# Hybrid conv and RWKV-7 layer on one core: key sums and low-rank products in fp32r pieces, and a later place for some weight remainders on VectorE

## The chip, the cores and the metric

The kernel runs on one core of a Trainium2 chip. The metric is the device time of one execution in microseconds. The profile is one execution of the program, with the engines TensorE (PE, its weight loads as PEld), VectorE (DVE), ScalarE (ACT), GpSimd (POOL) and SyncE (SP).

## The reference

One layer with 512 tokens, 16 learned meta tokens ahead of them (T = 528), model width 2048. All arithmetic is float32.

```python
h = rms_norm(concat([meta, x]), norm_mix_g)
p = h @ w_in                                   # 2048 -> 3072 conv columns + 3360 RWKV columns
y_conv = b_gate * conv3(c_gate * xc)           # 1024 channels
r, k, v, wd, ad, gd = split(token_shift(p[..., 3072:], mu))
w = -softplus(-(w0 + tanh(wd) @ w2)) - 0.5     # second low-rank stage: 64 -> 1024
decay = exp(-exp(w))
a = sigmoid(a0 + ad @ a2)                      # second low-rank stage: 64 -> 1024
g = sigmoid(gd) @ g2                           # 160 -> 1024
kk = k * k_k
kk = kk / max(norm(kk over each head of 64), 1e-12)
k = k * (1 + (a - 1) * k_a)
y = wkv7_scan(r, decay, k, v, -kk, kk * a)     # state S of 64 x 64 per head
y = (group_norm(y) * lnx_w + lnx_b + sum(r * k * r_k) * v) * g
h_res = h_res + concat([y_conv, y]) @ w_out
h_res = h_res + relu(rms_norm(h_res) @ w_up)**2 @ w_down
out = rms_norm(h_res)[meta tokens dropped]
```

## The kernel before

Features lie on the 128 partitions, tokens along the free dimension. Every dense product is made of three fp32r products: weights and activations are each cut into a rounded part (`w_hi`, `act_hi`) and a remainder (`w_lo`, `act_lo`), and TensorE adds hi·hi, hi·lo and lo·hi (`dense`, L1494). Small products (`ss`, `low`, `vtr`, gram and the rest) are plain fp32, which shows as two records each.

The 16 RWKV heads are worked off in 8 pairs (`pair(j)`, j = 0 to 7). While TensorE runs the dense projections of the next pair (six tiles of 16 k-steps, 96 k-steps in all, one k-step being three products of 528 columns), it runs the small steps of the present pair in between. `PACE` (L74) gives the order of the steps and how many k-steps stand ahead of each; the running totals that matter here are ss 2, low 7, vtr 12, ahead0 18, gram0 25, tr 28, gram1 31, and at the end var 93, ahead6 96.

Every engine walks the same list of steps in program order. At a step it does its own operations of that step and then the weight work that the total calls for: one quarter (4 k-steps of weights, 128 x 512) for each 4 k-steps. A quarter goes through three hands. SyncE loads it to `w_raw`, which holds 4 quarters (`load`, L447: the load of quarter q waits until the remainder of quarter q-4 is made). ScalarE rounds it to `w_hi` (`split`, L753). VectorE makes the remainder `w_lo` (`split`, L1063). In the text q5, q6, ... are the quarters of a pair, counted so that the dense work of the pair begins with q0; the engines run 6 quarters ahead, so that step "low" has the split of q6, "vtr" those of q7 and q8, "ahead0" q9, "gram0" q10 and q11, and "ahead6" the q5 of the next pair. For the steps in `SPLIT_FIRST` (low, base1, base2, y, var) an engine does the splits ahead of its operations, for the others behind; ScalarE has gram0 among the former too:

```python
            for name, k in zip(PACE, schedule()):
                if name not in ACT_SPLIT_FIRST:
                    steps_of(name)
                while splits < (96 if last and name == "var" else k) // KQ:
                    split(Q_PAIR + LEAD + splits, 24, j)
                    splits += 1
                if name in ACT_SPLIT_FIRST:
                    steps_of(name)
```

The steps around the change, in the names of the code:

- `ss`: squares of the keys (`fsq`, made by ScalarE in `square_keys`, L797) are summed over each head by a product with `same_head` (L1567, two halves of 264 columns). VectorE takes the sums (`ssm`, L1157), ScalarE the root, VectorE the reciprocal (L1160).
- `low`: the decay and learning-rate projections, four products with 64 rows each (L1573), one on the upper and one on the lower half of the array. ScalarE takes sigmoids (L861, L862), VectorE goes on with the scan (L1164) and what follows it.
- `vtr`: v is turned (L1578). VectorE does `kkn`, `tfac`, `kp` (L1176 to L1179).
- `ahead0`: VectorE scales the operands `at`, `b`, `bt`, `rt`, `kt` (L1182 to L1189).
- `gram0`: TensorE waits for `rt` (L1590). VectorE makes `rb` (L1191) and masks the result (`NA`, L1195). ScalarE rounds `rb` to `rb_hi` (`rbh`, L879), behind its splits of q10 and q11. GpSimd subtracts (`rbl`, L648) and masks `NA` (L653).
- `tr`: TensorE waits for the masked `NA`, turns bt and kt (L1595), then waits for `rbl` and sums `rb_hi` and `rb_lo` (L1598, L1599).
- `var`: variance and gate products (L1701, L1704), ScalarE's root (L913), VectorE's last four operations of the pair.

GpSimd loads the small weights of the next pair by its own DMA queue: `wa_w` once the products of `low` are done (L624, L625), `g_w` at the end of a pair. After the pairs come the output projection, the MLP and the final norm, which take about two thirds of the time and which the change leaves alone.

Of the kernel before, what the change touches and what calls it, by code (L numbers as in the profile page):

```python
# [31 lines left out]
P = 128  # L32
# [164 lines left out]
N_CONST = 4 + 6 + 4 + 5 + 3 + 4 + 2  # L197


def hybrid_layer(nc, x, meta, norm_mix_g, w_in, shift_mu, conv_w, decay_w0, decay_w2, iclr_a0, iclr_a2,  # L200
# [32 lines left out]
    same_head = sb("same_head", [P, P])  # L233
# [28 lines left out]
    KA = m_sb("KA", [P, 2, SLOTS, 2, C])  # L262
    AMV = m_sb("AMV", [P, 2, SLOTS, P])
    v_tok = m_sb("v_tok", [P, SLOTS, P])
    b_tok = m_sb("b_tok", [P, SLOTS, P])
    k_tok = m_sb("k_tok", [P, SLOTS, P])
# [9 lines left out]
    low_wa = m_sb("low_wa", [P, T])  # L276
    low_r = lambda name, n: sb(name, [P, n], F32R, on=mix)
    low_hi, low_lo, low_tail = low_r("low_hi", SEQ), low_r("low_lo", SEQ), low_r("low_tail", SEQ)
    wa_w = m_sb("wa_w", [P, P])
# [3 lines left out]
    rb_lo = low_r("rb_lo", SEQ)  # L283
# [8 lines left out]
    over_states.close()  # L292
    ZB = m_sb("ZB", [P, 7, P])
# [236 lines left out]
    def _(pool):  # L530
# [41 lines left out]
        const(nc.gpsimd.tensor_copy(same_head[:], blocks[:, 2, :]))  # L572
# [53 lines left out]

        def load_g(j):
# [4 lines left out]
        def pair(j, last=False):  # L632
# [7 lines left out]
            if not last:  # L640
                pool.wait_ge(pe_done, step(PE_STEPS, "low", j))
                load_wa(j + 1)

            if last:
                pool.wait_ge(z_done, at(6, 3, j))
                load_y(0, 1)
            pool.wait_ge(act_done, step(ACT_STEPS, "rbh", j))
# [12 lines left out]
            else:  # L660
                pool.wait_ge(dve_done, step(DVE_STEPS, "y4", j))
# [55 lines left out]
    def _(act):  # L717
# [86 lines left out]
        for n in range(6):  # L804
# [16 lines left out]
            if n == 1:  # L821
                act.wait_ge(z_done, 2)
                nc.scalar.activation(low_wa[0:HS, :], low_wa[0:HS, :], ACT.Tanh).then_inc(low_done, 1)
            if n == 2:
                act.wait_ge(z_done, 3)
                nc.scalar.activation(low_g[:, META:T], low_g[:, META:T], ACT.Sigmoid).then_inc(low_sig, 1)
                act.wait_ge(low_sig, 2)
# [12 lines left out]
        def pair(j, last=False):  # L840
# [13 lines left out]
            def steps_of(name):  # L854
# [56 lines left out]
                if name == "var":  # L911
                    pe("var")
# [921 lines left out]
```

## Time and profile before

| | |
|---|---|
| time, median of 3 runs | 2428.42 us (2427.71 to 2428.54) |
| the profiled execution's own time | 2427.97 us |
| its span | 2426.1 us |
| PE busy | 2401.2 us (99%) |
| PEld, DVE, ACT, POOL busy | 2034.1, 1130.0, 787.9, 206.5 us |
| TensorE's granted clock over the span | 0.997 |
| first `ss` of pairs 0 and 7 | 93.43 and 735.65 us |

The span runs from the first to the last instruction. The sum of the prediction is made against the profiled execution's own time. Starts of TensorE's instructions tell more than their durations here, since matmuls overlap and their ends are modelled.

### The profile page before, as it was taken

To read this page: it belongs to the slowest core of one execution; us is meant where nothing else is said; L and a number is where in the kernel's file an instruction comes from. 1 tells how busy PE (TensorE), PEld (TensorE's weight loads), DVE (VectorE), ACT (ScalarE), POOL (GpSimd) and SP (SyncE) were. 2 spreads that over 40 slices of the span, in tenths; PEclk is the share of its full clock that TensorE was granted. 3 is DMA by queue.
4 is the path that set the end of the run, shared out by engine and by line. 5 is a ranking of instruction groups with operands and counts; after the bars stand their busy time and mean duration, and the time that the engine had idled before them with its cause. 6 is when DMAs were issued, how large, how long until landed. Compare 5 with 4: busy or idle time off the path is not lost.

```text
span 2426.1 us, 42112 instructions
## 1 busy us (share of the span) xinstructions
PE 2401.2 (99%) x16524; PEld 2034.1 (84%) x16524; DVE 1130.0 (47%) x1733; ACT 787.9 (32%) x1329; POOL 206.5 (9%) x249
## 2 busy tenths in 40 slices
PE   8999999999999999999999999999999999999997
PEld 8999999999998788888888888888888888888886
DVE  7557657657657644433333333333332333333343
ACT  6534434434434322322222222221322322222333
POOL 6101101001002322000000000000000000000032
PEclk9999999999999999999999999999999999999998
DMA  8344244244244632333233333333332332332232
GB/s 248 81 98 103 68 101 103 69 105 101 70 102 116 190 107 79 96 105 96 82 110 92 90 97 96 88 105 87 87 108 84 99 101 84 100 104 87 87 100 92
DMA packets 487454, 243.68 MB, mean 100 GB/s; under 512 B 83294, under 2 KB 481120, under 8 KB 486880
## 3 DMA queue, kind: packets, MB, share of 16 engines
q1 hardware_dynamic: 470064, 219.99, 32.8%
q0 software_dynamic: 6720, 18.45, 2.4%
q10 hardware_dynamic: 10496, 2.62, 0.6%
q8 instruction: 145, 2.38, 0.4%
q14 instruction: 29, 0.24, 0.0%
HBM read 224.08 MB, written 16.92 MB: 99 GB/s over the span
## 4 chain that ended last, share of the span: by engine, by line
PE 89%; DVE 7%; ACT 1%; issue 1%; DMA 1%; SPq 0%; ACTq 0%; DVEq 0%
PE PD L1512 68%; PE PD L1517 13%; PE PD L1728 1%; DVE uni L1160 1%; DVE uni L1286 1%; DVE w_lo L1065 1%; PE PD L1541 1%; PE PW L1541 1%; PE PW L1690 1%; PE PW L1590 0%; PE PD L1446 0%; PE PW L1595 0%; DVE uni L1164 0%; PE PW L1654 0%; PE PW L1696 0%
## 5 line engine op out<-in xcount | busy, mean ns | idle before, releaser
L757 ACT CAST w_hi<-w_raw 128x512 fp32r<-128x512 f32 x780 | 457.6, 620 | 700.8 <-PE PD L1512 525.7
L1065 DVE TENSOR_TENSOR w_lo<-w_raw,w_hi 128x512 fp32r<-128x512 f32 x780 | 548.5, 736 | 293.0 <-ACT w_hi L757 289.8
L1512 PE MATMUL PD<-act_lo,w_hi 128*128 128x512 f32 x1344 | 531.3, 395 | 0.0
L1512 PE MATMUL PD<-act_hi,w_hi 128*128 128x512 f32 x1344 | 529.1, 394 | 0.0
L1512 PE MATMUL PD<-act_hi,w_lo 128*128 128x512 f32 x1344 | 528.6, 393 | 0.0
L1512 PE MATMUL PD<-u_hi,w_hi 128*128 128x512 f32 x1024 | 409.7, 400 | 0.0
L1512 PE MATMUL PD<-u_hi,w_lo 128*128 128x512 f32 x1024 | 403.3, 394 | 0.0
L1512 PE MATMUL PD<-u_lo,w_hi 128*128 128x512 f32 x1024 | 401.5, 392 | 0.0
L1512 PEld LDWEIGHTS PD<-act_hi,w_hi 128*128 128x128 f32 x1344 | 252.5, 188 | 61.7 <-issue 1.4
L1512 PEld LDWEIGHTS PD<-act_lo,w_hi 128*128 128x128 f32 x1344 | 252.1, 188 | 58.3 <-issue 0.2
L1512 PEld LDWEIGHTS PD<-act_hi,w_lo 128*128 128x128 f32 x1344 | 252.8, 188 | 57.3
L1418 DVE TENSOR_TENSOR res<-PD,res 128x512 f32<-128x512 f32 x128 | 88.5, 692 | 413.3 <-PE PD L1512 413.3
L1517 PE MATMUL PD<-act_hi,w_hi 128*128 128x264 f32 (+1 forms) x1248 | 266.2, 294 | 0.0
L1517 PE MATMUL PD<-act_hi,w_lo 128*128 128x264 f32 (+1 forms) x1248 | 251.3, 283 | 0.0
L1517 PE MATMUL PD<-act_lo,w_hi 128*128 128x264 f32 (+1 forms) x1248 | 251.1, 282 | 0.0
L1512 PEld LDWEIGHTS PD<-u_hi,w_lo 128*128 128x128 f32 x1024 | 192.2, 188 | 50.1
L1512 PEld LDWEIGHTS PD<-u_lo,w_hi 128*128 128x128 f32 x1024 | 192.3, 188 | 45.0
L1512 PEld LDWEIGHTS PD<-u_hi,w_hi 128*128 128x128 f32 x1024 | 192.3, 188 | 43.7
L1402 DVE SCALAR_TENSOR_TENSOR nt<-PD,rs 128x512 f32<-128x512 f32 x64 | 44.3, 692 | 366.5 <-PE PD L1512 366.2
L985 ACT ACTIVATE nt<-nt 128x512 f32<-128x512 f32 x64 | 40.6, 634 | 513.0 <-DVE nt L1402 513.0
L1517 PEld LDWEIGHTS PD<-act_hi,w_hi 128*128 128x128 f32 x1248 | 193.2, 189 | 12.6 <-issue 6.7
L1517 PEld LDWEIGHTS PD<-act_hi,w_lo 128*128 128x128 f32 x1248 | 192.2, 188 | 0.0
(319 smaller groups left out, 1880.5 us busy)
## 6 DMA issues: line engine op xcount, KB each, us to landing
w_raw<-in_w_up SPq DMA_DIRECT2D x256, 256.0 KB, 3.2
w_raw<-in_w_down SPq DMA_DIRECT2D x256, 256.0 KB, 2.9
w_raw<-in_w_in SPq DMA_DIRECT2D x200, 256.0 KB, 3.1
w_raw<-in_w_out SPq DMA_DIRECT2D x64, 256.0 KB, 2.7
residual<-res POOLq DMA_DIRECT2D x2, 2048.0 KB, 10.1
out<-rows SPq DMA_DIRECT2D x8, 512.0 KB, 5.3
yin<-mixed POOLq DMA_DIRECT2D x15, 256.0 KB, 3.6
x_rows<-in_x SPq DMA_DIRECT2D x3, 1024.0 KB, 7.4
```

The lines of the kernel that those rows point to most:

```text
L757: nc.scalar.copy(w_hi[:, q % RING], w_raw[:, q % RAW]).then_inc(hi_split, 1)
L985: nc.scalar.activation(nt, nt, ACT.Square).then_inc(u_sq, 1)
L1065: V.tensor_tensor(w_lo[:, q % RING], w_raw[:, q % RAW], w_hi[:, q % RING].bitcast(F32), ALU.subtract).then_inc(lo_split, 1)
L1160: done("inv", V.reciprocal(fsq, fsq))
L1286: done("inv2", V.reciprocal(ysq, ysq))
L1402: V.scalar_tensor_tensor(nt1[:, m % 3, :], pd_seq(n), 0.0, rs1[:], ALU.max, ALU.mult).then_inc(evacuated[n % 2], 1)
L1418: V.tensor_tensor(res[:, m, :], pd_seq(n), res[:, m, :], ALU.add).then_inc(evacuated[n % 2], 1)
L1512: ins = M(pd_seq(n), w, v[:, k, first:first + SEQ], start=begin, stop=end)
L1517: ins = M(PD[:, 2 * (n % 2) + a, cols], w, v[:, k, start:start + cols.stop - cols.start], start=begin, stop=end)
L1541: ins = M(bank[:, h, cols], w, v[:, k, start:start + cols.stop - cols.start], start=begin, stop=end)
L1690: ins = M(PW[:, (c - 1) % 2, 0:P], GT[:, c - 1, :], HB[:, 0, :] if c == 1 else ZB[:, c - 2, :], start=True, stop=True)
L1728: ins = M(PD[:, OUT_BANK[t], :], w, v[:, k, 0:SEQ], start=(k == 0 and i == 0), stop=(k == KT - 1 and i == 2))
```

## The change

The squared keys are cut into a rounded part `k_sq_hi` (ScalarE, right behind the square) and a remainder `k_sq_lo` (GpSimd, `split_squares`), and `ss` becomes four fp32r products with `same_head_r` in the place of two fp32 ones. ScalarE's `square_keys` for the next pair moves from step ahead6 to step var, ahead of the root. The plain `same_head` constant goes.

The low-rank weights `wa_w` are cut by GpSimd (`split_wa`, a cast and a subtraction of 128 x 128 for each pair, between the load of the next weights and `rbl`), the low-rank activations once at the start (`low_wa_hi` by ScalarE, `low_wa_lo` by VectorE), and `low` becomes twelve fp32r products in the place of four fp32 ones. `wa_w`, `rb_lo`, `k_sq_hi`, `k_sq_lo` and `low_wa` lie over other tiles of the mix, and ScalarE's `ktok` gets a wait on `wa_split` for that.

VectorE's splits move: q5 of the next pair from ahead6 to behind the operations of the next pair's `ss`, and q7 and q8 from behind `vtr` to behind the operations of `ahead0`, where q9 already was.

```diff
         def square_keys(j):
             act.wait_ge(z_done, at(5, 3, j))
             nc.scalar.activation(fsq, zk[:], ACT.Square, scale=p_("k_k", j)).then_inc(k_squared, 1)
+            act.wait_ge(k_squared, j + 1)
+            nc.scalar.copy(k_sq_hi[:], fsq).then_inc(k_sq_rounded, 1)
...
+        def split_squares(j):
+            pool.wait_ge(k_sq_rounded, j + 1)
+            nc.gpsimd.tensor_tensor(k_sq_lo[:], fsq, k_sq_hi[:].bitcast(F32), ALU.subtract).then_inc(k_sq_split, 1)
+
+        def split_wa(j):
+            pool.wait_ge(wa_loaded, 32 * (j + 1))
+            nc.gpsimd.tensor_copy(wa_hi[:], wa_w[:]).then_inc(wa_rounded, 1)
+            pool.wait_ge(wa_rounded, j + 1)
+            nc.gpsimd.tensor_tensor(wa_lo[:], wa_w[:], wa_hi[:].bitcast(F32), ALU.subtract).then_inc(wa_split, 1)
...
             if not last:
                 pool.wait_ge(pe_done, step(PE_STEPS, "low", j))
+                pool.wait_ge(wa_split, j + 1)
                 load_wa(j + 1)
...
+            if not last:
+                split_wa(j + 1)
             pool.wait_ge(act_done, step(ACT_STEPS, "rbh", j))
             done("rbl", nc.gpsimd.tensor_tensor(rb_lo, ld[:, 0:SEQ], rb_hi.bitcast(F32), ALU.subtract))
...
             if last:
                 load_y(*range(6, KT - 1))
             else:
+                split_squares(j + 1)
                 pool.wait_ge(dve_done, step(DVE_STEPS, "y4", j))
...
                     done("btok", nc.scalar.copy(b_tok[:].rearrange("p c n -> p (c n)"), in_row(0)))
+                    if not last:
+                        act.wait_ge(wa_split, j + 2)
                     done("ktok", nc.scalar.copy(k_tok[:].rearrange("p c n -> p (c n)"), in_row(1)))
...
                 if name == "var":
+                    if not last:
+                        square_keys(j + 1)
                     pe("var")
                     done("std", nc.scalar.activation(ysq, PW[:, 0, :], ACT.Sqrt, bias=eps_t[:, 1:2]))
-                if name == "ahead6" and not last:
-                    square_keys(j + 1)
...
-            splits, tiles, y_split = 0, 0, 0
+            splits, tiles, y_split = -1 if j else 0, 0, 0
             for name, k in zip(PACE, schedule()):
                 if name not in SPLIT_FIRST:
                     steps_of(name)
-                while splits < (96 if last and name == "var" else k - 4 if last and name in ("amv", "ahead5") else k) // KQ:
+                held = 2 if name == "vtr" else 1 if name == "ahead6" and not last or last and name in ("amv", "ahead5") else 0
+                while splits < (96 if last and name == "var" else k) // KQ - held:
                     split(Q_PAIR + LEAD + splits, 24, j)
                     splits += 1
...
                 if name == "ss":
-                    pe.wait_ge(k_squared, j + 1)
-                    for a in range(2):
-                        ins = M(PW[:, 2 + a, 0:HALF], same_head[:], half(fsq, a), start=True, stop=True)
+                    for i, (made, squares) in enumerate(((k_sq_rounded, k_sq_hi), (k_sq_split, k_sq_lo))):
+                        pe.wait_ge(made, j + 1)
+                        for a in range(2):
+                            ins = M(PW[:, 2 + a, 0:HALF], same_head_r[:], half(squares[:], a), start=(i == 0), stop=(i == 1))
                 if name == "low":
-                    pe.wait_ge(wa_loaded, at(32, 32, j))
+                    pe.wait_ge(wa_split, j + 1)
                     dve("ssm")
                     for a in range(2):
-                        for h in range(2):
-                            ins = M(PW[:, 2 * h + a, 0:HALF], wa_w[hs[h], :], half(low_wa[hs[h], :], a), start=True, stop=True)
+                        for i, (w, v) in enumerate(((wa_hi, low_wa_hi), (wa_lo, low_wa_hi), (wa_hi, low_wa_lo))):
+                            for h in range(2):
+                                ins = M(PW[:, 2 * h + a, 0:HALF], w[hs[h], :], half(v[hs[h], :], a), start=(i == 0), stop=(i == 2))
```

## Rows read from the trace of the kernel before

**Rows 1.** The page's first part: busy time, share of the span, instructions.

```profile
PE 2401.2 (99%) x16524; PEld 2034.1 (84%) x16524; DVE 1130.0 (47%) x1733; ACT 787.9 (32%) x1329; POOL 206.5 (9%) x249
```

**Rows 2.** Timeline of PE in pair 0: start, duration, instruction, output and inputs.

```profile
93.19 0.40 PE L1517 MATMUL PD<-act_hi,w_lo 128*128 128x260 f32 x2
93.43 1.05 PE L1567 MATMUL PW<-uni,same_head 128*128 128x264 f32 x4
...
94.56 0.40 PE L1517 MATMUL PD<-act_lo,w_hi 128*128 128x260 f32 x2
...
97.65 0.39 PE L1517 MATMUL PD<-act_hi,w_lo 128*128 128x260 f32 x2
...
99.41 0.40 PE L1517 MATMUL PD<-act_lo,w_hi 128*128 128x260 f32 x2
```

**Rows 3.** Timeline of PE, the first `ss` of pairs 1 and 2.

```profile
184.81 0.83 PE L1567 MATMUL PW<-uni,same_head 128*128 128x264 f32 x3
...
276.61 0.83 PE L1567 MATMUL PW<-uni,same_head 128*128 128x264 f32 x3
```

**Rows 4.** Waits in pair 1 (184.8 to 214 us): total us, times, longest.

```profile
PEld PW L1590 <- DVE ar L1188: 0.3, 1, 0.3
PEld PW L1595 <- DVE NA L1195: 0.3, 1, 0.3
```

**Rows 5.** Timeline of PE in pair 1, around step `tr`.

```profile
208.45 0.77 PE L1595 MATMUL PW<-ident,bt 128*128 128x128 f32 x5
...
209.84 0.40 PE L1599 MATMUL PW<-rb_lo,same_head_r 128*128 128x512 f32 x1
```

**Rows 6.** Timeline of DVE, one row of pair 0, then pair 1; idle before in brackets.

```profile
107.82 1.29 DVE L1065 TENSOR_TENSOR w_lo<-w_raw,w_hi 128x512 fp32r<-128x512 f32 x2 [1.84 <-ACT w_hi L757]
...
187.74 0.69 DVE L1065 TENSOR_TENSOR w_lo<-w_raw,w_hi 128x512 fp32r<-128x512 f32 x1
...
199.03 0.71 DVE L1179 TENSOR_TENSOR uni<-zk,uni 128x528 f32<-128x528 f32 x1
200.55 1.29 DVE L1065 TENSOR_TENSOR w_lo<-w_raw,w_hi 128x512 fp32r<-128x512 f32 x2 [0.81 <-ACT w_hi L757]
201.76 0.70 DVE L1182 SCALAR_TENSOR_TENSOR ar<-uni 128x528 f32<-128x528 f32 x1
...
205.45 0.69 DVE L1065 TENSOR_TENSOR w_lo<-w_raw,w_hi 128x512 fp32r<-128x512 f32 x1
...
206.84 1.56 DVE L1195 TENSOR_TENSOR NA<-PW,gram_mask 128x640 f32<-128x640 f32 x2
208.43 2.22 DVE L1065 TENSOR_TENSOR w_lo<-w_raw,w_hi 128x512 fp32r<-128x512 f32 x2
```

**Rows 7.** Timeline of ACT in pair 1, and at `var` of the same pair.

```profile
199.83 1.15 ACT L757 CAST w_hi<-w_raw 128x512 fp32r<-128x512 f32 x2
...
204.28 0.62 ACT L757 CAST w_hi<-w_raw 128x512 fp32r<-128x512 f32 x1 [1.24 <-DMA w_raw<-in_w_in]
206.84 0.62 ACT L879 CAST rb_hi<-uni 128x512 fp32r<-128x512 f32 x1 [1.94 <-DVE uni L1191]
...
273.19 0.69 ACT L913 ACTIVATE uni<-PW,eps_t 128x512 f32<-128x512 f32 x1 [2.30 <-PE PW L1704]
```

**Rows 8.** Timeline of POOL in pair 1.

```profile
191.34 0.53 POOL L625 DMA_DIRECT2D wa_w<-in_iclr_a  x1
207.55 1.28 POOL L648 TENSOR_TENSOR rb_lo<-uni,rb_hi 128x512 fp32r<-128x512 f32 x1 [15.69 <-ACT rb_hi L879]
208.79 4.40 POOL L653 TENSOR_TENSOR uni<-NA,level_mask 128x320 f32<-128x320 f32 x4
```

**Rows 9.** DMA issues of the whole program: KB each, median us to landing.

```profile
wa_w<-in_iclr_a POOLq DMA_DIRECT2D x8, 32.0 KB, 2.9
```

**Rows 10.** Two POOL lines: duration in ns, minimum, median, maximum, and forms.

```profile
L573 POOL CAST same_head_r<-blocks x1: 290/290/290, 15.3 to 15.3; 128x128 fp32r<-128x128 f32 x1
...
L653 POOL TENSOR_TENSOR uni<-NA,level_mask x32: 881/1141/1373, 116.3 to 763.1; 128x320 f32<-128x320 f32 x32
```

More of the change, by code:

```diff
@@ L196 @@
 T_END = T_MLP + FFG * 24
-N_CONST = 4 + 6 + 4 + 5 + 3 + 4 + 2
+N_CONST = 4 + 6 + 4 + 4 + 3 + 4 + 2
 def hybrid_layer(nc, x, meta, norm_mix_g, w_in, shift_mu, conv_w, decay_w0, decay_w2, iclr_a0, iclr_a2,
@@ L232, in hybrid_layer @@
     ones = sb("ones", [P, P])
-    same_head = sb("same_head", [P, P])
     same_head_r = sb("same_head_r", [P, P], F32R)
@@ L262, in hybrid_layer @@
     KA = m_sb("KA", [P, 2, SLOTS, 2, C])
+    over_pairs = ExitStack()
+    k_sq_lo = sb("k_sq_lo", [P, T], F32R, on=over_pairs)
+    over_pairs.close()
+    over_pairs = ExitStack()
+    low_wa = sb("low_wa", [P, T], on=over_pairs)
+    over_pairs.close()
     AMV = m_sb("AMV", [P, 2, SLOTS, P])
     v_tok = m_sb("v_tok", [P, SLOTS, P])
+    over_b = ExitStack()
+    rb_lo = sb("rb_lo", [P, SEQ], F32R, on=over_b)
+    over_b.close()
     b_tok = m_sb("b_tok", [P, SLOTS, P])
+    over_k = ExitStack()
+    wa_w = sb("wa_w", [P, P], on=over_k)
+    over_k.close()
     k_tok = m_sb("k_tok", [P, SLOTS, P])
@@ L275, in hybrid_layer @@
     cu = m_sb("cu", [P, T + 2])
-    low_wa = m_sb("low_wa", [P, T])
     low_r = lambda name, n: sb(name, [P, n], F32R, on=mix)
     low_hi, low_lo, low_tail = low_r("low_hi", SEQ), low_r("low_lo", SEQ), low_r("low_tail", SEQ)
-    wa_w = m_sb("wa_w", [P, P])
+    low_wa_hi, low_wa_lo = low_r("low_wa_hi", T), low_r("low_wa_lo", T)
+    wa_hi, wa_lo = low_r("wa_hi", P), low_r("wa_lo", P)
     g_w = m_sb("g_w", [P, P])
@@ L282, in hybrid_layer @@
     g_hi, g_lo, g_tail = low_r("g_hi", P), low_r("g_lo", P), low_r("g_tail", P)
-    rb_lo = low_r("rb_lo", SEQ)
     ar = m_sb("ar", [P, 2, TP])
@@ L292, in hybrid_layer @@
     over_states.close()
+    over_last_states = ExitStack()
+    k_sq_hi = sb("k_sq_hi", [P, T], F32R, on=over_last_states)
+    over_last_states.close()
     ZB = m_sb("ZB", [P, 7, P])
@@ L354, in hybrid_layer @@
     wa_loaded, g_loaded = sem("wa_loaded"), sem("g_loaded")
+    wa_rounded, wa_split = sem("wa_rounded"), sem("wa_split")
     low_done, low_sig, low_top = sem("low_done"), sem("low_sig"), sem("low_top")
@@ L358, in hybrid_layer @@
     z_done, k_squared, key_made = sem("z_done"), sem("k_squared"), sem("key_made")
+    k_sq_rounded, k_sq_split = sem("k_sq_rounded"), sem("k_sq_split")
     conv_step = sem("conv_step")
@@ L680, in _ @@
         load_g(0)
+        split_wa(0)
+        split_squares(0)
         for j in range(PAIRS - 1):
@@ L822, in _ @@
                 act.wait_ge(z_done, 2)
-                nc.scalar.activation(low_wa[0:HS, :], low_wa[0:HS, :], ACT.Tanh).then_inc(low_done, 1)
+                nc.scalar.activation(low_wa[0:HS, :], low_wa[0:HS, :], ACT.Tanh).then_inc(low_sig, 1)
+                act.wait_ge(low_sig, 2)
+                nc.scalar.copy(low_wa_hi[:], low_wa[:]).then_inc(low_top, 1)
             if n == 2:
@@ L826, in _ @@
                 nc.scalar.activation(low_g[:, META:T], low_g[:, META:T], ACT.Sigmoid).then_inc(low_sig, 1)
-                act.wait_ge(low_sig, 2)
+                act.wait_ge(low_sig, 3)
                 nc.scalar.copy(low_hi[:], low_g[:, META:T]).then_inc(low_top, 1)
@@ L1124, in _ @@
                 V.tensor_tensor(low_tail[r, :], low_g2[r, META:T], low_tail[r, :].bitcast(F32), ALU.subtract).then_inc(low_done, 1)
+                dve.wait_ge(low_top, 2)
+                V.tensor_tensor(low_wa_lo[:], low_wa[:], low_wa_hi[:].bitcast(F32), ALU.subtract).then_inc(low_done, 1)
             if n == 4:
-                dve.wait_ge(low_top, 2)
+                dve.wait_ge(low_top, 3)
                 V.tensor_tensor(low_lo[:], low_g[:, META:T], low_hi[:].bitcast(F32), ALU.subtract).then_inc(low_done, 1)
```

1 line of the change is left out of this document (removed).

## The prediction

> **What bounds the kernel.** I read the busy shares first: PE is busy for 2401.2 of 2426.1 us [rows 1], so only what TensorE issues, or a new wait of TensorE, can move the time. Its starts come next, because the ends of matmuls are modelled. In the dense work two products of 260 and 256 columns start 0.24 us apart from the next two (93.19 to 93.43) [rows 2], or 0.119 us for each; this holds through nearly all of a pair. Then I looked for the places where TensorE just meets another engine. Pair 0 takes 184.81 - 93.43 = 91.38 us, pair 1 takes 276.61 - 184.81 = 91.80 us [rows 2, 3]. Both have the same instructions, so pair 1 holds 0.42 us of waiting that pair 0 lacks. The waits name the places: gram0's weight load waits for VectorE's `rt`, and tr's for the masked `NA` [rows 4]. So VectorE between the scan and `NA` is on the edge of being the bound in every pair but the first, and any change of 0.1 us on TensorE or VectorE counts there. The last look is at the timelines of VectorE, ScalarE and GpSimd in pair 1 [rows 6 to 8].
>
> **ss on TensorE.** The fp32 form starts at 93.43 and the second dense group behind it at 94.56 [rows 2]; less the 0.24 us of the first dense group, it costs 0.89 us. Four fp32r products of 264 columns continue the dense pattern at 0.119 us x 264/258 = 0.122 us each, 0.49 us. Gain 0.40 us in each pair. Its inputs: the cast of `k_sq_hi` (some 0.62 us, as ScalarE's cast of a quarter) and the square (0.7) now run where ScalarE waits 2.30 us for the products of var [rows 7], so they are hidden; without that cover they would delay the root by 1.3 us. GpSimd's subtraction takes about 1.3 us (`rbl` [rows 8]). From 270.89, where that wait began, the three end near 273.6, and `ss` starts at 276.61 [rows 3]: a margin of 3 us hides them.
>
> **low on TensorE.** From 97.65 to 99.41, less two dense groups of 0.24 us, the fp32 form costs 1.28 us [rows 2]. Its eight records run two by two, the upper and the lower half of the array together, four times 0.22 us as in ss, so 0.40 us is entry and exit. Twelve fp32r products run as six couples: 6 x 0.122 + 0.40 = 1.13 us, a gain of 0.16. No row shows fp32r products of 64 rows. If they don't overlap they cost 12 x 0.122 + 0.40 = 1.86, a loss of 0.58. I take the couples, since the nearest rows are fp32 products of the same shape that do overlap. Together TensorE is 0.56 us shorter in each pair, 0.02 us longer at the other bound.
>
> **The moved remainders: what comes earlier.** q5 now goes behind ss: `ssm` starts at 187.74 rather than 0.6 us later, which keeps low, now reached 0.40 us earlier, free of a wait. The reciprocal also ends 0.6 us earlier, but q5 and q6 then stand ahead of `ld`, one split more than q6 alone, and a second split costs 1.29 - 0.69 = 0.60 us [rows 6]. So from the scan on nothing is earlier or later. At vtr, `kp` ends at 199.74 and VectorE waits 0.81 us for ScalarE's cast of q7 before it makes q7 and q8 and gets to `at` at 201.76 [rows 6]. Without these two, `at` starts at 199.77. From `at` to the split behind `kt` the five operations take 205.45 - 201.76 = 3.69 us, so that split, now of q7, starts at 203.46; `rt` is ready 2 us earlier and gram0's wait is gone. Two splits at 0.61 us, then the stretch of one split and `rb` ahead of the masks (206.84 - 205.45 = 1.39) and the masks' 1.56 follow: `NA` starts at 206.07 and ends at 207.63 instead of 208.40, and tr can start 0.77 us earlier.
>
> **The moved remainders: what comes later.** `w_raw` holds four quarters, so the load of q11 waits for the remainder of q7. Before, q7's split starts at 200.55 and the cast of q11 at 204.28, where ScalarE had waited 1.24 us for that very DMA [rows 6, 7]: 3.73 us from the one to the other. Now q7's split starts at 203.46, so the cast of q11 starts at 207.19. At gram0 ScalarE does its splits first, so `rbh` is queued behind this cast: it starts 0.53 us later (two casts take 1.15, one 0.62 [rows 7]), 207.72, and ends 208.34, where it was 207.46. `rbl` follows with its old lag of 0.09 and its 1.28 us [rows 8]: 209.71. TensorE would start L1599 1.39 us behind the start of tr, as before, at 209.07 (207.68 + 1.39 [rows 5]). But L1598 can only start at about 209.77, and L1599 follows 0.33 later (512 columns at the dense rate, 0.23, and 0.1 for a weight load that nothing covers) at 210.10, against 209.84 before [rows 5]. What the shorter products and the missing waits gain is all spent waiting for `rb_lo`, and 0.26 us more. Behind tr ScalarE's `btok`, VectorE's bonus and the rest are tied to TensorE as before.
>
> **Two contentions on top.** VectorE's two splits at 208.43 take 2.22 us beside GpSimd's L648 and L653, two such splits alone 1.29; the GpSimd operation takes from 881 to 1373 ns [rows 6, 8, 10]. So a VectorE subtraction of two SBUF tiles and a GpSimd operation on SBUF wait for each other. Now q10 and q11 are split from 207.66 and from 208.27 to 208.96 (1.59 us behind the start of `NA`, as before, and 0.61 more), and `rbl` is asked for at 208.43, in the middle of the second. By the stretch seen on L653 it loses up to 0.5 us; I take 0.35, the rest of that split less its write-out, with 0 and 0.5 as bounds. Second, `split_wa`: its load is issued at 191.34 and takes 2.9 us [rows 8, 9], so a cast of 0.29 us [rows 10] and a subtraction of about 0.32 (a quarter of `rbl`) fall at 194.3 to 195.6, onto VectorE's scan and the short operations behind it, which lead straight to q7's split. Delay between 0 and 0.6 us; I take the middle, 0.3. In pair 7 there is no `split_wa`. The Trainium skill (SBUF — State Buffer, "Who interferes with whom") speaks against this change: a VectorE instruction with two SBUF inputs and a GpSimd instruction that reads SBUF contend, and the one that starts first holds the shared port for its whole length. By that rule both delays occur and the sum is +5.5 us; without it the sum is the late DMA's alone, +1.3 us. The trace agrees so far as the 2.22 against 1.29 us go.
>
> **Pair 0 and the rest.** In pair 0 VectorE is 1.4 us further ahead of TensorE (q7's split starts at 107.82, 14.39 us behind `ss`, against 15.74 in pair 1 [rows 2, 3, 6]). The same steps there put the end of `rbl` over 1 us ahead of its use, so it keeps its 0.56. At the start, square, cast and subtraction of the first keys (some 2.7 us) have the dense tile of v to hide behind, 96 products at 0.122 = 11.7 us, and the cuts of `low_wa` and `wa` stand ahead of that; without this cover the first `ss` would be some 2 us late once. One constant less on GpSimd is nothing. The output projection and the MLP are unchanged.
>
> **Sum.** Pair 0: -0.56. Pairs 1 to 7: 0.26 + 0.35 = 0.61 each, 4.27. Pairs 1 to 6: 0.30 more, 1.80. Together +5.5 us on 2427.97: 2433.5. The profiled execution lies 0.45 under the median of the runs, which is no more than their spread, so I leave it.
>
> **Rivals.**
> - *The late DMA alone, hardly any contention* (0.29): 7 x 0.26 - 0.56 = +1.3, 2429.2. For it: `rbl` is asked for only 0.16 us behind the start of q11's split, and the cut of `wa` may find VectorE between operations. Against it: the 2.22 us.
> - *The reordering works and nothing is late* (0.13), the other sign: the cast of q11 isn't in the way of `rbh`, because its load lands sooner or is free sooner. Then pairs gain the products and the waits: 8 x 0.56 + 7 x 0.42 = 7.4, 2420.6. It decides itself at one point: `rbl` must end by about 208.7 in pair 1's times, 1.0 us sooner than worked out. Against it stands ScalarE's wait of 1.24 us for exactly this load.
> - *fp32r products of 64 rows don't overlap* (0.15, beside any of the cases): in pairs 1 to 7 the wait for `rb_lo` hides it; in pair 0 it costs 0.7.
> - *The forecast, late DMA with both contentions*: 0.58. Its own range is 2431.5 (no delay by `split_wa`: 7 x 0.61 - 0.56 = +3.7) to 2436.5 (both delays at their upper bound: 6 x 1.36 + 0.76 - 0.56 = +8.4).
>
> **Range and chances.** 2427.5 to 2436.5 leaves out the faster rival (0.13) and the far upper end. What a measurement can tell from no change is 0.2%, 4.9 us, so the line to slower lies at 2433.3, just under the forecast. Of the forecast's 0.58 some two fifths (0.23) lie below the line; of the late DMA alone, 0.27 below and 0.02 above it: faster 0.13, same 0.50, slower 0.37.
>
> **What would show it.** ss: L1567 at a spacing of 0.12 us, four records. low: twelve records in couples. In pair 1 counted from its first ss: q7's split near 18.7, the cast of q11 near 22.4 with a DMA as its releaser, `rbh` right behind it, L1598 waiting on POOL `rb_lo`; pairs of 92.2 to 92.8 us against 91.80, pair 0 near 90.8. If L1598 has no wait and pairs take about 90.8 us, the step on the load of q11 is wrong. If POOL's L648 stays at 1.28 us and the scan at 1.26, the contentions are.

## The result, and the profile after

The changed kernel takes 2436.37 us (median of 7 runs, 2436.10 to 2437.36); the kernel before takes 2428.42 us in its 7 runs beside them (2427.23 to 2429.31). The ratio is 1.0033 [1.0024, 1.0043]: 8 us slower. The profiled executions are 2436.10 and 2427.97 us. The forecast was 2433.5 with its own range of 2431.5 to 2436.5, so the time lies 0.1 us inside the upper end.

The page's first part of the kernel after, to set beside [rows 1]:

```profile
PE 2399.9 (99%) x16556; PEld 2034.4 (84%) x16556; DVE 1126.9 (46%) x1734; ACT 791.6 (33%) x1338; POOL 221.3 (9%) x272
```

TensorE is busy 1.3 us less, and the kernel is 8 us longer: the products became shorter, as meant, and waiting took their place. The timeline of PE in pair 1 around `ss` and `low` (start, duration, instruction, output and inputs):

```profile
185.09 0.41 PE L1606 MATMUL PW<-k_sq_hi,same_head_r 128*128 128x264 f32 x2
185.34 0.41 PE L1606 MATMUL PW<-k_sq_lo,same_head_r 128*128 128x264 f32 x2
185.59 0.40 PE L1555 MATMUL PD<-act_hi,w_hi 128*128 128x260 f32 x2
...
188.95 0.41 PE L1555 MATMUL PD<-act_hi,w_lo 128*128 128x260 f32 x2
189.28 0.39 PE L1613 MATMUL PW<-low_wa_hi,wa_hi 64*128 64x264 f32 x2
189.51 0.28 PE L1613 MATMUL PW<-low_wa_hi,wa_lo 64*128 64x264 f32 x2
189.63 0.29 PE L1613 MATMUL PW<-low_wa_lo,wa_hi 64*128 64x264 f32 x2
...
190.00 0.29 PE L1613 MATMUL PW<-low_wa_lo,wa_hi 64*128 64x264 f32 x2
190.22 0.52 PE L1555 MATMUL PD<-act_hi,w_hi 128*128 128x260 f32 x2
190.57 0.40 PE L1555 MATMUL PD<-act_lo,w_hi 128*128 128x260 f32 x2
```

`ss` occupies 185.09 to 185.59, 0.50 us, with 0.12 us for each of its four products: the 0.49 of the forecast. In `low` the starts of the rows lie 0.12 us apart (the first two 0.23), and each row is two products, one on the upper and one on the lower 64 rows of the array: fp32r products of 64 rows do overlap. From the last dense group to the second one behind (188.95 to 190.57), less two groups of 0.24, `low` costs 1.14 us: the forecast's 1.13.

The place where the time goes is step `tr`. Timelines of PE, ACT, POOL and DVE there, in pair 1:

```profile
208.18 0.77 PE L1635 MATMUL PW<-ident,bt 128*128 128x128 f32 x5
208.78 0.71 PE L1635 MATMUL PW<-ident,kt 128*128 128x128 f32 x5
210.62 0.50 PE L1638 MATMUL PW<-rb_hi,same_head_r 128*128 128x512 f32 x1 [1.14 <-POOL rb_lo L675]
210.96 0.39 PE L1639 MATMUL PW<-rb_lo,same_head_r 128*128 128x512 f32 x1
...
207.69 0.62 ACT L787 CAST w_hi<-w_raw 128x512 fp32r<-128x512 f32 x1 [4.17 <-DMA w_raw<-in_w_in]
208.22 0.61 ACT L913 CAST rb_hi<-uni 128x512 fp32r<-128x512 f32 x1
...
193.55 0.83 POOL L647 CAST wa_hi<-wa_w 128x128 fp32r<-128x128 f32 x1 [1.65 <-DMA wa_w<-in_iclr_a]
194.46 0.52 POOL L649 TENSOR_TENSOR wa_lo<-wa_w,wa_hi 128x128 fp32r<-128x128 f32 x1
208.91 1.66 POOL L675 TENSOR_TENSOR rb_lo<-uni,rb_hi 128x512 fp32r<-128x512 f32 x1 [13.93 <-ACT rb_hi L913]
...
194.70 1.39 DVE L1201 TENSOR_TENSOR_SCAN uni<-carry,uni 128x528 f32<-128x528 f32 x1
...
203.98 1.89 DVE L1100 TENSOR_TENSOR w_lo<-w_raw,w_hi 128x512 fp32r<-128x512 f32 x3
205.79 0.74 DVE L1228 SCALAR_TENSOR_TENSOR uni<-zr,par,uni 128x512 f32<-128x512 f32 x1
206.57 1.55 DVE L1232 TENSOR_TENSOR NA<-PW,gram_mask 128x640 f32<-128x640 f32 x2
208.16 1.29 DVE L1100 TENSOR_TENSOR w_lo<-w_raw,w_hi 128x512 fp32r<-128x512 f32 x2
```

Read it from the wait backwards. L1638 sits idle 1.14 us for `rb_lo`. That subtraction takes 1.66 us, where the same one took 1.28 before [rows 8], and runs beside VectorE's split of the last quarters from 208.16. It waits for `rb_hi` (208.22), which is queued behind the cast of q11 (207.69), which sat idle 4.17 us for the load of its quarter (1.24 before [rows 7]). The load waits for the remainder of q7, now the first of the three splits at 203.98. The whole span has the same wait seven times, in pairs 1 to 7. From the waits of PE over the pairs (total us, times, longest):

```profile
PE PW L1638 <- POOL rb_lo L675: 7.9, 7, 1.1
PE PW L1635 <- DVE NA L1232: 0.5, 2, 0.3
```

Counted from each pair's own first `ss` (184.81 before, 185.09 after), pair 1 compares so:

| us behind the first `ss` | before | forecast | after |
|---|---|---|---|
| first split behind `kt` (q7's, after) | 20.64 | 18.65, or 18.95 with `split_wa` | 18.89 |
| cast of q11 | 19.47 | 22.4, or 22.7 | 22.60 |
| start of `tr` | 23.64 | 22.87, or 23.17 | 23.09 |
| second sum of `rb` | 25.03 | 25.94 | 25.87 |

The time between first `ss` products, for the whole program, from the profiled executions:

| stretch | before | after | forecast of the difference | measured |
|---|---|---|---|---|
| start to first `ss` | 93.43 | 94.06 | 0 | +0.63 |
| pair 0 | 91.38 | 91.04 | -0.56 | -0.34 |
| pairs 1 to 6, sum | 550.84 | 556.40 | +5.46 | +5.56 |
| pair 7, first `ss` to second sum of `rb` | 25.02 | 25.65 | +0.61 | +0.63 |
| from there to the MLP's norm product | 221.79 | 221.02 | 0 | -0.77 |
| from there to the start of TensorE's last product | 1429.67 | 1431.97 | 0 | +2.30 |

The pairs gave +5.85 us of a forecast +5.5. The rest, +2.2 us net, lies where nothing was foreseen, and most of it in the MLP. The rows of pair 7 and of the stretch behind it belong together: +0.63 and -0.77 make -0.14, so the late sum of the last pair was made up behind it, and +5.1 us of the pairs' +5.85 reach the end of the program.

In this document "the MLP" is the last row: it begins at the norm product in front of the MLP and ends with TensorE's last start; behind that both executions have 14.0 us.

### The profile page after: what moved, and what is told of

The parts are those of the page before. It is cut to its first block, busy times and chain, and to the rows that moved or that the text cites. A ratio compares the mean times of both kernels' runs of the same rounds, so it can differ in the third digit from the quotient of the medians.

```text
span 2434.1 us, 42216 instructions
## 1 busy us (share of the span) xinstructions
PE 2399.9 (99%) x16556; PEld 2034.4 (84%) x16556; DVE 1126.9 (46%) x1734; ACT 791.6 (33%) x1338; POOL 221.3 (9%) x272
## 4 chain that ended last, share of the span: by engine, by line
PE 86%; DVE 8%; DMA 3%; ACT 1%; issue 1%; POOL 0%; SPq 0%; ACTq 0%; DVEq 0%
PE PD L1550 67%; PE PD L1555 11%; PE PD L1768 1%; DMA w_raw<-in_w_in 1%; DVE uni L1197 1%; DVE uni L1323 1%; DVE w_lo L1100 1%; PE PD L1579 1%; PE PW L1579 1%; PE PW L1730 1%; DMA UU<-gram 0%; DMA gram<-NA 0%; DVE uni L1201 0%; PE PW L1694 0%; PE PW L1736 0%
## 5 line engine op out<-in xcount | busy, mean ns | idle before, releaser
L1100 DVE TENSOR_TENSOR w_lo<-w_raw,w_hi 128x512 fp32r<-128x512 f32 x780 | 541.2, 728 | 298.1 <-ACT w_hi L787 295.1
L1550 PEld LDWEIGHTS PD<-act_hi,w_lo 128*128 128x128 f32 x1344 | 252.8, 188 | 59.8 <-issue 2.8
L1550 PEld LDWEIGHTS PD<-act_lo,w_hi 128*128 128x128 f32 x1344 | 252.1, 188 | 58.3 <-issue 0.2
L1555 PEld LDWEIGHTS PD<-act_lo,w_hi 128*128 128x128 f32 x1248 | 192.5, 188 | 0.0
```

The source lines that it names most:

```text
L1100: V.tensor_tensor(w_lo[:, q % RING], w_raw[:, q % RAW], w_hi[:, q % RING].bitcast(F32), ALU.subtract).then_inc(lo_split, 1)
L1550: ins = M(pd_seq(n), w, v[:, k, first:first + SEQ], start=begin, stop=end)
L1555: ins = M(PD[:, 2 * (n % 2) + a, cols], w, v[:, k, start:start + cols.stop - cols.start], start=begin, stop=end)
```

## The experiments

Each run's ratio is to runs of the kernel before on the same chip, and the column behind the time is the difference of the two medians. Times of different rows should be compared by that column, since the kernel before itself has medians of 2427.50 to 2428.71 us beside them. The table has the stretches of the profiled executions that the text below uses; the rest of each text is its edit, its expectation and the reading.

| kernel | time, us | to before beside it | ratio [95%] | pair 0 | pairs 1 to 6, mean | last `rb` sum to MLP norm | MLP |
|---|---|---|---|---|---|---|---|
| before | 2428.42 | | | 91.38 | 91.81 | 221.8 | 1429.67 |
| after | 2436.37 | +7.95 | 1.0033 [1.0024, 1.0043] | 91.04 | 92.73 | 221.0 | 1431.97 |
| after, again | 2433.82 | +6.32 | 1.0029 [1.0018, 1.0040] | 90.88 | 92.59 | 220.7 | 1430.97 |
| rbh first | 2428.59 | +0.63 | 0.9999 [0.9990, 1.0008] | 90.97 | 91.49 | 223.5 | 1431.06 |
| q7 back at vtr | 2432.90 | +4.94 | 1.0022 [1.0013, 1.0031] | 91.00 | 92.21 | 223.4 | 1430.53 |
| no splits moved | 2432.46 | +4.50 | 1.0019 [1.0010, 1.0028] | 91.14 | 92.06 | 223.7 | 1429.62 |
| splits moved only | 2431.64 | +4.14 | 1.0018 [1.0009, 1.0027] | 91.38 | 92.38 | 220.7 | 1429.68 |
| squares and moves | 2431.05 | +3.09 | 1.0014 [1.0005, 1.0023] | 90.96 | 92.44 | 220.7 | 1429.69 |
| rbh first, `wa` cut later | 2425.95 | -1.55 | 0.9995 [0.9986, 1.0004] | 91.33 | 91.19 | 223.0 | 1430.72 |
| the same, again | 2426.73 | -1.19 | 0.9993 [0.9984, 1.0002] | 91.06 | 91.32 | 222.9 | 1431.57 |
| squares, rbh first | 2422.09 | -5.41 | 0.9978 [0.9969, 0.9987] | 90.98 | 91.07 | 221.2 | 1429.45 |
| the same, again | 2422.30 | -5.62 | 0.9977 [0.9968, 0.9986] | 90.96 | 91.10 | 221.9 | 1429.28 |
| the same, without a tile | 2422.45 | -5.47 | 0.9980 [0.9971, 0.9989] | 90.96 | 91.02 | 222.1 | 1429.21 |
| fp32 `low`, all else | 2423.57 | -5.14 | 0.9980 [0.9971, 0.9989] | 90.99 | 91.16 | 221.9 | 1429.64 |

**rbh first.** ScalarE does `rbh` ahead of its splits at gram0, so the late cast of q11 no longer stands before it.

```diff
-ACT_SPLIT_FIRST = SPLIT_FIRST + ("gram0",)
+ACT_SPLIT_FIRST = SPLIT_FIRST
```

> The changed kernel with one edit: at gram0 ScalarE rounds rb (rbh) ahead of its casts of q10 and q11 instead of behind them. Theory (the cast of q11 waits for a late load and holds rbh back): the wait of TensorE's L1638 for rb_lo (1.14 us in pair 1) goes, the masked NA becomes what tr waits for, at about 23.1 us behind the first ss, so pairs 1 to 6 take 91.2 us instead of 92.7 and GpSimd's rb_lo takes 1.28 us instead of 1.66. That is 7 x 1.5 = 10 us less than the changed kernel, about 2426. Rival (rb_lo is late for another reason, GpSimd's own order or contention with VectorE): pairs stay above 92.3 us and the time stays within 2 us of the changed kernel's 2436.4.

The time fell to 2428.59 us, 0.6 us over the kernel before beside it where the kernel after was 8.0 over, and the wait for `rb_lo` is gone from the waits of PE. GpSimd's `rb_lo` takes 1.28 to 1.30 us again in every pair. Nothing was done to the load or to VectorE's order, so the pairs' loss came through the place of `rbh` behind the late cast, with what `rb_lo` lost to VectorE's split because it was late. It stayed 2.6 us above the expectation. What is left over the pairs, in its waits:

```profile
PE PD L1768 <- DVE act_lo L1170: 1.4, 2, 0.9
PE PW L1658 <- DMA uni<-inverse: 1.1, 2, 0.6
PE PW L1664 <- DVE uni L1295: 1.1, 2, 0.9
PE PW L1635 <- DVE NA L1232: 0.5, 2, 0.3
```

All but the last are later points (the triangular inverse that goes through DRAM, and the last pair's normed output) that the wait at `tr` had partly covered: in the kernel after `act_lo` costs 0.5 us and `uni` 0.4 there. The longest of them lie in pair 7.

**q7 back at vtr.** VectorE makes q7's remainder at vtr again, and only q8's behind ahead0.

```diff
-                held = 2 if name == "vtr" else 1 if name == "ahead6" and not last or last and name in ("amv", "ahead5") else 0
+                held = 1 if name == "vtr" else 1 if name == "ahead6" and not last or last and name in ("amv", "ahead5") else 0
```

> The changed kernel with q7's remainder back at vtr and only q8's held until behind the scaled operands. Theory: q11's load is then free at once (cast of q11 near 19.6 us behind the first ss, no wait of L1638), but VectorE waits for the cast of q7 again, gets to the operand `at` 1.3 us later, and NA is ready near 23.7: pairs 1 to 6 take 91.9 us, close to the 91.80 of the kernel before, and the time is about 2430. Rival (the late load is not what matters, the moves cost by VectorE's order alone): pairs stay near 92.7 us.

The wait for `rb_lo` goes here too, with the load freed early and ScalarE's order untouched, which is the same link cut from its other end. In its place stands the one that the kernel before had (waits of PE over the pairs):

```profile
PE PW L1635 <- DVE NA L1232: 4.7, 7, 0.7
PE PW L1630 <- DVE ar L1225: 1.3, 5, 0.3
```

VectorE waits at vtr for ScalarE's cast again, and in pairs 1 to 7 the second mask of `NA` starts 22.98 to 23.13 us behind `ss` where it started at 22.77 before. Pairs take 92.2 us, against 91.9 expected. The time came out 2.9 us above the expectation: the pairs took more than foreseen, and so did the stretch behind the last `rb` sum (+1.6 us against before) and the MLP (+0.9).

**No splits moved.** The kernel after with both products, and VectorE's splits where they were before.

```diff
-            splits, tiles, y_split = -1 if j else 0, 0, 0
+            splits, tiles, y_split = 0, 0, 0
...
-                held = 2 if name == "vtr" else 1 if name == "ahead6" and not last or last and name in ("amv", "ahead5") else 0
+                held = 0 if name == "vtr" else 1 if last and name in ("amv", "ahead5") else 0
```

> The changed kernel with all of VectorE's remainders back in their old places (q5 at ahead6, q7 and q8 at vtr): the fp32r products alone. Theory: TensorE's shorter products are swallowed by the wait for VectorE's NA at tr, which is as late as before plus the 0.2 us that GpSimd's split of the low-rank weights costs the scan: pairs 1 to 6 take 91.9 to 92.0 us, pair 0 91.0, time 2429 to 2431. Rival (TensorE is the bound in every pair): pairs take 91.25 us, 4 us less than the kernel before, 2424.

Pairs take 92.06 us, 0.25 more than before, though TensorE's products of `ss` and `low` are 0.54 us shorter in each: its waits are for `ar` (3.5 us in seven). So shorter products were worth nothing here; TensorE only arrives sooner at VectorE, the bound between the scan and `NA`. The cut of `wa` is in this run too and makes the scan longer or later in four of the pairs 1 to 6, so the 0.25 us may be its share, as the expectation had it; no run has the products without it and without the moves. This run too lies above its expectation, by 1.9 us in the stretch behind the last `rb` sum.

**Splits moved only.** The kernel before with the diff's `splits` and `held` lines and nothing else.

> The kernel before with nothing but the moved remainders of VectorE (q5 behind ss, q7 and q8 behind the scaled operands); all small products fp32 as before. Theory (the late load of q11 and rb_lo's loss to the split of q11 are the whole cost, and TensorE's shorter products only add to the waiting): cast of q11 near 22.35 us behind the first ss, rb_lo takes 1.6 to 1.8 us, its second product (rb_lo's matmul) starts at 25.65 instead of 25.03, pairs 1 to 6 take 92.4 us, pair 0 stays at 91.4, and the time is 4.4 us above the kernel before, 2432.5. Rival (the moves only hurt because TensorE arrives earlier in the changed kernel): pairs stay at 91.8, no difference.

2431.64 us, 4.1 us over the kernel before beside it, where 4.4 were expected. The pairs' mean rises by 0.58 us with no product changed and no `split_wa`. The scan stays at 1.26 us. That is the late load and `rb_lo`'s stretch by themselves; `rb_lo` (duration in ns: minimum, median, maximum) shows a spread that it had not before, when it took 1.28 to 1.29 us in every pair:

```profile
L648 POOL TENSOR_TENSOR rb_lo<-uni,rb_hi x8: 1256/1492/1768, 115.2 to 763.4; 128x512 fp32r<-128x512 f32 x8
```

**Squares and moves.** The kernel before with the squares as four fp32r products and the moved splits; `low` stays fp32, and nothing cuts `wa`.

> The kernel before with only the squared keys as four fp32r products and the moved remainders; low stays fp32, so GpSimd has no split of the low-rank weights. Theory (that split delays VectorE's scan by 0.2 us, which goes on to q7's remainder and rb_lo): the scan takes 1.26 us again, pairs 1 to 6 take 92.45 instead of 92.70 us although low is 0.15 us longer on TensorE, and pair 0 takes 0.15 us more. In all 1.3 us less than the changed kernel, about 2435. Rival (GpSimd's split is free, shorter products count): pairs take 92.85 us, the time is 1 us above the changed kernel.

Pairs take 92.44 us, 0.63 over before, as the steps without `split_wa` give (0.61). They aren't alike: the load of q11 lands at different times, so `rbh` starts between 22.69 us (pair 2, which takes 91.83 us) and 23.99 us behind `ss` (pair 6, 93.12 us). The total came out 4 us under what was expected, because nothing was lost outside the pairs: the MLP is at 1429.69, and the stretch behind the last `rb` sum is 1.1 us shorter, by as much as that sum came later in pair 7.

**rbh first, `wa` cut later.** The kernel after with both orders turned: ScalarE's `rbh` ahead of its splits, and GpSimd's `split_wa` behind `rbl`.

```diff
-            if not last:
-                split_wa(j + 1)
             pool.wait_ge(act_done, step(ACT_STEPS, "rbh", j))
             done("rbl", nc.gpsimd.tensor_tensor(rb_lo, ld[:, 0:SEQ], rb_hi.bitcast(F32), ALU.subtract))
+            if not last:
+                split_wa(j + 1)
```

> The changed kernel with two edits: ScalarE's rbh ahead of its casts of q10 and q11, and GpSimd's split of the low-rank weights behind rb_lo instead of ahead of it. Theory (that split, at 8.4 to 9.9 us behind the first ss, holds up VectorE's ld and scan by 0.2 to 0.35 us, and with rbh first this goes straight to the masked NA, which is what tr waits for): scan starts at 9.5 and takes 1.26 us in all pairs, NA ends near 22.8, pairs take 91.0 us instead of 91.25 to 91.6, 1.5 to 2 us less than with rbh first alone, about 2426.5. Rival (the split is harmless there, or costs as much behind rb_lo): no difference from rbh first alone, 2428.6 within 0.7.

2425.95 us, as expected, and 2426.73 in a second run: 1.6 and 1.2 us under the kernel before beside them. The scan is 1.26 us in all pairs and starts 9.51 us behind `ss` in pairs 1 to 7. In the kernel after it either takes 1.39 us from 9.61 on, as in pair 1, or starts at 9.88; only in pair 7, which has no `split_wa`, is it at 9.51 with 1.26. So the cut of `wa` costs VectorE's chain 0.23 to 0.37 us (11.00 or 11.14 us for the end of the scan, against 10.77).

**Squares, rbh first.** The squares and moves, with `rbh` ahead of ScalarE's splits.

> The kernel before with the squared keys as four fp32r products, the moved remainders and rbh first on ScalarE; low stays fp32 and GpSimd splits no low-rank weights. Theory: nothing delays VectorE, NA ends near 22.8 and is ready when TensorE comes (22.87), so pairs take 91.0 us and the time is 5 to 6 us less than the kernel before, about 2423. Rival (the block inverse behind gram0, whose copies back from DRAM TensorE awaits at x16, becomes the next bound when pairs get shorter): pairs of 91.3 to 92, time within 2.5 us of the kernel before.

2422.09 us, 5.4 us under the kernel before beside it, as expected: the version to keep. Timelines of PE, ACT and POOL at `tr`, pair 1:

```profile
208.30 0.71 PE L1612 MATMUL PW<-ident,kt 128*128 128x128 f32 x5
208.76 0.48 PE L1615 MATMUL PW<-rb_hi,same_head_r 128*128 128x512 f32 x1
...
206.09 0.62 ACT L894 CAST rb_hi<-uni 128x512 fp32r<-128x512 f32 x1 [3.56 <-DVE uni L1206]
206.74 1.14 ACT L770 CAST w_hi<-w_raw 128x512 fp32r<-128x512 f32 x2
...
206.79 1.28 POOL L659 TENSOR_TENSOR rb_lo<-uni,rb_hi 128x512 fp32r<-128x512 f32 x1 [15.16 <-ACT rb_hi L894]
```

`rb_lo` ends at 208.07, 0.7 us ahead of the start of L1615, and takes 1.28 us again: it is under way before VectorE's splits of q10 and q11 start at 207.67. L1615 has no wait. Pairs of 91.02 us, which five of the six take, are 0.79 under before: 0.40 from `ss`, and the rest is the 0.42 of waiting that each pair but the first had.

**After, again.** The kernel after, unaltered, beside the two last.

> The changed kernel once more, unaltered. Theory (the pairs give 5.2 us of the difference, and the rest, 0.6 us ahead of the first ss and 2.3 us in the MLP, is variation between executions): pairs 92.6 to 92.8 again, but the MLP stretch differs from the 1432.0 us of the first profile by 1 us or more, and the time may come out at 2434 to 2437. Rival (the MLP part belongs to the program, by where its code lies): again 1431.5 to 1432.5 us and 2436.4 within 0.7.

2433.82 us with ratio 1.0029: the kernel is slower, by 6.3 us here and by 8.0 in the first runs, and the two medians differ by 2.5 us. The pairs repeat (92.59 against 92.73 us); the start of the last stretch and the MLP don't quite (1430.97 against 1431.97).

**Where the remaining 4 us lie.** All kernels made from the one after had 1 to 2 us more in the MLP, behind the last pair, or in both; those made from the one before had not. Four runs looked for the cause. The first takes the best kernel and drops the plain `same_head` tile (512 bytes) as the change does, so that every later tile lies lower:

```diff
-N_CONST = 4 + 6 + 4 + 5 + 3 + 4 + 2
+N_CONST = 4 + 6 + 4 + 4 + 3 + 4 + 2
-    same_head = sb("same_head", [P, P])
-        const(nc.gpsimd.tensor_copy(same_head[:], blocks[:, 2, :]))
```

> The squares with rbh first, as in the run that was faster than both kernels (2422.1 us), but without the 512-byte tile same_head, which the changed kernel leaves out: every later tile lies 512 bytes lower. Open is why all kernels built on the changed one take 1 to 2 us more in the MLP, and why the inverse of the first pair comes back from DRAM some 1.7 us later. Theory, the addresses: the MLP behind its norm takes 1430.5 to 1432 us in the profiled execution instead of 1429.5, and pair 0 waits 0.16 us or more at t16: 2423 to 2424.5 us. Rival, the second low-rank stage as twelve products or variation between executions: MLP 1429.5, no wait at t16, 2422 us.

> The squares with rbh first once more, unaltered, on the same chip: 2422.1 us, MLP 1429.5 us in the profiled execution. If the MLP takes over 1430.5 us here, then the length of the MLP varies between executions and is no property of a kernel.

> The kernel with all products, rbh first and the cut of wa behind rbl, once more (2425.95 us before). It differs from the run without the tile by the second low-rank stage alone. If the stage as twelve products costs time behind the pairs or in pair 0, this run stays near 2426 us with the run without the tile at 2422; if the addresses do, both lie above 2423.5; if it is variation, both may come out at 2422 to 2424.

2422.45 us without the tile against 2422.30 with it, and MLP 1429.21 against 1429.28: a shift by 512 bytes is not the cause, and the last run below, which keeps every tile where the kernel after has it, leaves the addresses out altogether. The kernel with all products stays at 2426.73, so variation between executions doesn't account for it either: `low` as twelve products costs 4 us together with its cuts. The last run takes only the twelve products away and leaves the cuts of `wa` and `low_wa` in place; the sum is then of the rounded tops alone.

```diff
-                        for i, (w, v) in enumerate(((wa_hi, low_wa_hi), (wa_lo, low_wa_hi), (wa_hi, low_wa_lo))):
-                            for h in range(2):
-                                ins = M(PW[:, 2 * h + a, 0:HALF], w[hs[h], :], half(v[hs[h], :], a), start=(i == 0), stop=(i == 2))
+                        for h in range(2):
+                            ins = M(PW[:, 2 * h + a, 0:HALF], wa_hi[hs[h], :].bitcast(F32), half(low_wa_hi[hs[h], :].bitcast(F32), a), start=True, stop=True)
```

> All of the changed kernel with rbh first and the cut of wa behind rbl (2425.95 and 2426.73 us in its two runs), but TensorE does the second low-rank stage as four fp32 products again, of the rounded tops wa_hi and low_wa_hi: the remainders wa_lo and low_wa_lo are still made, and left out of the sum. Only TensorE's program differs. Open is where some 4 us against the squares alone (2422.1, 2422.3) come from: 1.3 to 2.4 us in the MLP, up to 1.8 behind the last pair's rb_lo, 0.2 to 0.8 in the pairs. Theory, TensorE's program with the twelve products: without them the MLP takes 1429.5 us in the profiled execution, the pairs 91.02, and the time is 2422 us. Rival, what the other engines do more (ScalarE's cast and VectorE's remainder of low_wa, GpSimd's cut of wa, the place of the load): it stays near 2426 us, with the MLP above 1430.5.

2423.57 us, 5.1 us under the kernel before beside it. The MLP is back at 1429.64 and the stretch before it at 221.9. The three runs of the squares lie 5.4, 5.6 and 5.5 us under theirs, the two with twelve products 1.6 and 1.2. So of the 4 us between the two kinds some 3.8 belong to TensorE's twelve products and some 0.4, which is within the noise, to the cuts of other engines. The intervals of the ratios with and without the products overlap a little (0.9993 [0.9984, 1.0002], 0.9980 [0.9971, 0.9989]), so the size is less sure than the sign.

The traces show where in the MLP the time goes. It is a loop, one turn of which takes 179 us and has 768 weight loads, which follow each other every 0.23 us. Some turns have pauses that no release explains, and those over 0.15 us lie at two places only: at the first load of a turn, and 11 loads further on. Timelines of PEld as the second turn begins, first in the kernel after (1168.34 is the first place, 1171.41 the second), then in the kernel before (1162.92 and 1165.36):

```profile
1168.34 0.19 PEld L1550 LDWEIGHTS PD<-act_hi,w_hi 128*128 128x128 f32 x1 [0.16 <-issue]
...
1170.57 0.19 PEld L1550 LDWEIGHTS PD<-act_lo,w_hi 128*128 128x128 f32 x1
1171.41 0.19 PEld L1550 LDWEIGHTS PD<-act_hi,w_lo 128*128 128x128 f32 x1 [0.65 <-issue]
```

```profile
1162.92 0.19 PEld L1512 LDWEIGHTS PD<-act_hi,w_hi 128*128 128x128 f32 x1 [0.45 <-issue]
...
1165.12 0.19 PEld L1512 LDWEIGHTS PD<-act_lo,w_hi 128*128 128x128 f32 x1
1165.36 0.19 PEld L1512 LDWEIGHTS PD<-act_hi,w_lo 128*128 128x128 f32 x1
```

Pauses at the first place occur in both kinds. At the second place they occur in all seven profiled executions with twelve products, in one to six turns, 0.4 to 2.8 us in all, and in none of the seven without. The MLP takes 1430.5 to 1432.0 us in six of the first seven and 1429.2 to 1429.7 in the others. The kernel with no splits moved, at 1429.62, has the twelve products too; it has the pause at the second place in one turn, 0.42 us, and none at the first.

A second row goes with the products in the same way, the landing time of the inverse's way to DRAM (KB each, median us to landing), first with twelve products (the kernel of 2426.73), then with fp32 ones:

```profile
inverse<-UU SPq DMA_DIRECT2D x16, 80.0 KB, 3.2
```

```profile
inverse<-UU SPq DMA_DIRECT2D x16, 80.0 KB, 2.6
```

It is 3.0 to 3.2 us in all seven profiled executions with twelve products and 2.6 in all seven without.

## Why the prediction was right, and where not

- **The products.** `ss` 0.89 to 0.50 us (0.49 forecast), `low` 1.28 to 1.14 (1.13). The rival that 64-row fp32r products don't overlap fell by the starts 0.12 us apart (its bound for `ss` and `low` together should have been 0.18 us longer, 0.58 less 0.40, and not 0.02; nothing rests on it). The hidden square and cast at var, and GpSimd's subtraction, cost nothing in any pair: `ss` has no wait in the waits of PE. In pair 0 the gain reached 0.34 of 0.56 us: it was 0.50 up to the inverse's products, and 0.16 of it went into waiting there.
- **What comes earlier.** q7's split 18.89 us behind `ss` against 18.95 with `split_wa`, and `tr` at 23.09 against 23.17. That the gap before gram0 disappears was right too.
- **What comes later.** q11's cast follows q7's split by 3.71 us (3.73 forecast), and the second sum of `rb` starts at 25.87 (25.94). The two runs that cut this link at different ends, rbh first and q7 back at vtr, each removed the wait for `rb_lo`, and the moves alone brought it (5.2 us in seven pairs). It is shown.
- **`rb_lo`'s stretch.** 1.66 us in pair 1 and a median of 1.59 over all pairs against 1.28: +0.38 and +0.31 for a forecast of 0.35. It stays between 1.27 and 1.31 in the kernels where it starts before VectorE's splits do (before, both with `rbh` first and `wa` later or none, q7 back at vtr, no splits moved), and in pair 2 of the squares and moves, where it came early, 1.27. Pairs 1, 3, 4 and 5 of that run, in which it is asked for during the split of q11, have 1.67 to 1.82; pairs 6 and 7, in which it is asked for only as that split ends, have 1.26. The end says it more clearly than the duration: in pairs 1, 4, 5 and 6 of the kernel after `rb_lo` ends 25.48 us behind `ss`, 1.12 behind the end of q11's split, whether it is asked for at 23.82 or at 23.92.
- **`split_wa`.** 0.23 to 0.37 us in VectorE's chain, forecast 0.3. The page that the forecast drew on, the Trainium skill (SBUF — State Buffer, "Who interferes with whom"), agrees with both stretches: by it the sum was +5.5 us and without it +1.3, and the pairs gave +5.85.
- **The other rivals.** The late DMA alone (+1.3) falls with the two stretches. The reordering without anything late did not happen, but its size was not far off: squares, moves and `rbh` first lie 5.4 us under the kernel before, where the rival had 7.4 with `low` in it.
- **The terms that were mis-sized: "The output projection and the MLP are unchanged", and pair 7.** The MLP was costed at 0 and gave +2.30 us; the first `ss` came 0.63 us late, which is within what executions differ by, since that start scatters between 93.30 and 94.51 us over all kernels. Pair 7 was costed at +0.61 like the others and gave -0.14 with the stretch behind it, since later waits of that pair shrank, among them the one for `act_lo`, from 0.9 to 0.5 us. The MLP's part goes with TensorE's twelve products: the last run took it away with them, and the pauses at the second place of the loop divide the fourteen profiled executions without exception. How products in the pairs bring pauses to a later, unchanged loop was not found. The profile names no releaser for them, and no run changed the length of TensorE's program without changing its work, which would be the next test.
- **How much of it was luck.** The mechanism gave +5.85 us in the pairs for +5.5, by the steps that were forecast. The time is 2.9 us over the forecast of 2433.5 and stayed in the range by 0.1 us, which is no more than the rounding of the bound (2427.97 + 8.36 is 2436.3, not 2436.5); that the unforeseen part was no larger is luck. The same kernel took 2433.82 us when it ran again.

What stays open besides: why the inverse's transfer lands 0.5 us later with twelve fp32r products than with four fp32 ones.

## What to carry to other kernels

When a remainder or a copy is moved later to clear the way of its own engine, follow the buffer that it frees: here the load, the cast behind it and a small cast queued behind that one reached TensorE five steps on, and changing the order of two casts on ScalarE turned a loss of 8 us into 0.6. Shorter products are worth nothing in front of an engine that is already the bound, and then each 0.1 us that a helper engine takes from it through a shared access shows in full. A saving of 0.15 us a pair (`low`) that needs three cuts on three engines and more instructions lost 4 us in all; take out each part of a change by itself before keeping it.

## What the runs showed of the hardware that was not expected

- Twelve fp32r products with 64 rows in the place of four fp32 ones, in 8 pairs (32 more recorded TensorE instructions of 16,524), came with pauses of TensorE's weight loads at one place of an unchanged loop (0.4 to 2.8 us in all, in seven of seven executions against none of seven), with an MLP 0.9 to 2.3 us longer than before in six of these seven, and with 3.0 to 3.2 us instead of 2.6 for a transfer of 80 KB between SBUF and DRAM.
- GpSimd's subtraction of 128 x 512 takes 1.28 us when it begins before VectorE's subtraction of two SBUF tiles, even where the two then overlap (206.79 to 208.07 beside a split from 207.67), and 1.4 to 1.8 us when it is asked for during one. Whoever comes second pays: the two splits take 2.23 us there, beside `rb_lo` and the masks behind it, and 1.29 in the kernel after.
- A cast of 128 x 128 on GpSimd takes 0.29 us by itself [rows 10] and 0.83 in pair 1 of the kernel after, where it is asked for during VectorE's splits of q5 and q6 (192.93 to 194.22) and ends at 194.38.
